# Bias addition and row maximum of the biased attentions in one VectorE instruction per token tile

## What is computed

```
a, b:  logits = q . k * 64**-0.5 + bias[head, bucket(t - s)],  -1e30 where s > t
l:     logits = q . k * 96**-0.5,                              -1e30 where s > t
p = softmax(logits);  o = p @ v            (b: p0 - lambda * p1)
```

## Time and profile before

| | before |
|---|---|
| median of three runs | 1180.93 us (1180.62 to 1181.59) |
| profiled execution, span from first to last instruction | 1175.5 us |
| around the span, against that median | 5.4 us |
| TensorE matmuls busy | 1127.3 us (96%) |
| VectorE busy | 746.6 us (64%), 997 instructions |
| ScalarE busy | 570.9 us (49%), 761 instructions |
| mean granted TensorE clock | 0.992 |

### The profile page before, as it was taken

One profiled execution on the slowest core, in us unless ns is written; L12 is line 12 of the kernel. 1 busy time (PEld: TensorE's weight loads), 2 busy tenths in 40 slices (PEclk: granted clock), 3 DMA queues, 4 the chain that ended last, 5 costly groups with the idle time before them and its releaser, 6 DMA issues.

```text
span 1175.5 us, 22572 instructions
## 1 busy us (share of the span) xinstructions
PE 1127.3 (96%) x9889; PEld 1071.8 (91%) x9889; DVE 746.6 (64%) x997; ACT 570.9 (49%) x761; POOL 76.0 (6%) x137
## 2 busy tenths in 40 slices
PE   7999999999999999999799999999998989999998
PEld 7787879879999999988688999999986789999998
DVE  4656867357465556767888756555587675665563
ACT  5445556344444434585345544343475554544443
POOL 2221011100000000400000000000020000000000
PEclk9999999999999999999899999999999999999999
DMA  6953354424555555534000555455554215455551
GB/s 253 337 160 108 144 180 180 149 102 173 179 187 180 180 183 193 192 141 144 1 3 3 184 180 188 180 180 184 190 201 143 73 60 188 183 180 180 181 189 61
DMA packets 30238, 185.04 MB, mean 157 GB/s; under 512 B 3579, under 2 KB 6848, under 8 KB 9148
## 3 DMA queue, kind: packets, MB, share of 16 engines
q1 hardware_dynamic: 24464, 174.07, 41.2%
q0 software_dynamic: 2464, 7.11, 2.1%
q10 hardware_dynamic: 3212, 2.42, 0.7%
HBM read 180.18 MB, written 3.41 MB: 156 GB/s over the span
## 4 chain that ended last, share of the span: by engine, by line
PE 75%; DVE 9%; ACT 6%; issue 4%; DMA 3%; POOL 2%; ACTq 0%; SPq 0%; DVEq 0%; POOLq 0%
PE bank L664 74%; ACT w_hi L2184 2%; DVE w_lo L1411 2%; DMA w_raw<-in_weights 2%; ACT exps L2284 1%; DMA bias<-bias_rows 1%; DVE stats L1606 1%; PE bank L843 1%; DVE logits L1598 1%; DVE inverse L2074 0%; PE bank L678 0%; DVE inverse_t L2099 0%; DMA bias_rows<-bias_lines 0%; POOL inverse_rms_diagonals L2672 0%; PE bank L1105 0%
## 5 line engine op out<-in xcount | busy, mean ns | idle before, releaser
L1411 DVE TENSOR_TENSOR w_lo<-w_raw,w_hi 128x2048 fp32r<-128x2048 f32 x160 | 364.8, 2291 | 194.7 <-ACT w_hi L2184 194.5
L2184 ACT ACTIVATE w_hi<-w_raw 128x2048 fp32r<-128x2048 f32 x164 | 312.0, 1913 | 110.7 <-DMA w_raw<-in_weights 105.2
L664 PE MATMUL bank<-x_channels_hi,w_hi 128*128 128x256 f32 x1424 | 231.7, 286 | 9.1 <-ACT w_hi L2184 3.5
L664 PE MATMUL bank<-x_channels_lo,w_hi 128*128 128x256 f32 x1424 | 229.1, 284 | 0.0
L664 PE MATMUL bank<-x_channels_hi,w_lo 128*128 128x256 f32 x1424 | 221.0, 278 | 0.0
L664 PEld LDWEIGHTS bank<-x_channels_hi,w_hi 128*128 128x128 f32 x1424 | 196.8, 192 | 12.5 <-ACT w_hi L2184 3.8
L664 PEld LDWEIGHTS bank<-x_channels_lo,w_hi 128*128 128x128 f32 x1424 | 194.9, 191 | 0.0
L664 PEld LDWEIGHTS bank<-x_channels_hi,w_lo 128*128 128x128 f32 x1424 | 191.5, 189 | 0.0
L664 PE MATMUL bank<-hidden_hi,w_lo 128*128 128x256 f32 x528 | 103.3, 284 | 0.0
L664 PE MATMUL bank<-hidden_hi,w_hi 128*128 128x256 f32 x528 | 102.0, 280 | 0.0
L664 PE MATMUL bank<-hidden_lo,w_hi 128*128 128x256 f32 x528 | 101.7, 279 | 0.0
(11 more groups left out here) (436 smaller groups left out, 1546.8 us busy)
## 6 DMA issues: line engine op xcount, KB each, us to landing
w_raw<-in_weights SPq DMA_DIRECT2D x164, 1024.0 KB, 4.8
bias_rows<-bias_lines POOLq DMA_DIRECT2D x3, 768.0 KB, 4.4
mem_rows<-in_mem POOLq DMA_DIRECT2D x2, 1024.0 KB, 5.2
bias<-bias_rows ACTq DMA_DIRECT2D x1, 1536.0 KB, 14.1
xn<-in_x SPq DMA_DIRECT2D x1, 1024.0 KB, 4.9
out<-xn SPq DMA_DIRECT2D x4, 256.0 KB, 2.5
wide_masks<-in_triangle_masks POOLq DMA_DIRECT2D x1, 832.0 KB, 6.5
bias<-bias_rows ACTq DMA_DIRECT2D x1, 768.0 KB, 5.5
```

What stands on the lines that cost most here:

```text
L664: return nc.tensor.matmul(out, lhs, rhs, start=start, stop=stop)
L1411: V.tensor_tensor(k.w_lo[:, s, :], k.w_raw[:, s, :], k.w_hi[:, s, :].bitcast(F32), ALU.subtract).then_inc(k.lo_done, 1)
L2184: A.activation(k.w_hi[:, s, :], k.w_raw[:, s, :], ACT.Copy).then_inc(k.hi_done, 1)
```

## The change

The two steps of VectorE become one instruction per token tile, `tensor_tensor_reduce`: out = (logits + bias) * (-scale), and beside it the minimum of `out` along the columns, started at 3e38, into `stats`. The stored logits are therefore negated, and the minimum is the negated maximum that the exponentials take as their bias; their scale becomes -1. Since the scale now multiplies the bias too, the one-hot matrix is multiplied by 8 when ScalarE copies it (64**-0.5 = 1/8); the mask -1e30 stays large whatever its factor, in "l" as well. The signal `biased` is gone: its waits, of TensorE before it overwrites a logits bank and before the turns of "mem" and after "b" and "l", are for `maxed`. The wait for the output of head h-4, which frees the `stats` slot, now stands ahead of the bias addition. The unbiased attentions keep their code.

```diff
@@ tensor_program, attention (twice) @@
-                    PE.wait_ge(*(k.biased if bias else k.exped).at(tag, i - 2))
+                    PE.wait_ge(*(k.maxed if bias else k.exped).at(tag, i - 2))
...
@@ tensor_program (also .all("b"), .all("l")) @@
-            turns("mem", (0, 1), k.biased.at("a", 6), k.biased.at("a", 7), k.mem_normed.all("mem"))
+            turns("mem", (0, 1), k.maxed.at("a", 6), k.maxed.at("a", 7), k.mem_normed.all("mem"))
...
@@ vector_program, attention, maxima @@
                 b, scale = bank[4 + h % 2], k.scale_of(tag)
+                if h >= 4 and step == 1:
+                    V.wait_ge(*k.o.at(tag, h - 4))
                 if bias:
                     if h >= 2:
                         V.wait_ge(*k.exped.at(tag, h - 2))
-                    L = k.lbuf[:, h % 2, 0:total]
...
-                    V.scalar_tensor_tensor(out=L, in0=b[:, 0:total], scalar=scale, in1=k.head_bias(tag, h), op0=ALU.mult,
-                                           op1=ALU.add).then_inc(k.biased.sem, 1)
-                    V.wait_ge(*k.biased.at(tag, h))
+                    for tok in range(NT):
+                        cols = slice(off[tok], off[tok] + spans[tok])
+                        r = V.tensor_tensor_reduce(out=k.lbuf[:, h % 2, cols], in0=b[:, cols], in1=k.head_bias(tag, h)[:, cols],
+                                                   scale=-scale, scalar=HUGE, op0=ALU.add, op1=ALU.min,
+                                                   accum_out=stat(h)[:, tok:tok + 1])
+                        if tok == 0:
+                            k.dve.mark(r)
+                    r.then_inc(k.maxed.sem, 1)
+                    continue
...
@@ scalar_program, attention, exponentials @@
-                                     scale=1.0 if bias else k.rstd_cols("cross")[:, tok:tok + 1] if tag == "c" else k.scale_of(tag),
+                                     scale=-1.0 if bias else k.rstd_cols("cross")[:, tok:tok + 1] if tag == "c" else k.scale_of(tag),
...
@@ scalar_program @@
-    A.activation(k.hot_r[:, :], k.hot[:, :], ACT.Copy).then_inc(k.act_once.sem, 1)
+    A.activation(k.hot_r[:, :], k.hot[:, :], ACT.Copy, scale=8.0).then_inc(k.act_once.sem, 1)
```

More of the change, by code:

```diff
@@ L23 @@
 NEG = -1e30
+HUGE = 3e38
 EPS = 1e-6
@@ L285, in signals @@
         self.qk = Signal(nc, "logits_made", **heads)
-        self.biased = Signal(nc, "logits_biased", **{n: heads[n] for n, a in att.items() if a[2]})
         self.maxed = Signal(nc, "logits_maxed", **heads)
@@ L828, in attention @@
                     if h >= 2:
-                        PE.wait_ge(*(k.biased if bias else k.exped).at(tag, h - 2))
+                        PE.wait_ge(*(k.maxed if bias else k.exped).at(tag, h - 2))
                 for tok in range(NT):
@@ L942, in tensor_program @@
     attention("b", beside_b)
-    PE.wait_ge(*k.biased.all("b"))
+    PE.wait_ge(*k.maxed.all("b"))
     PE.wait_ge(*k.pt.all("b"))
@@ L1136, in tensor_program @@
     attention("l", lambda i: warm(8, 0) if i == 0 else None)
-    PE.wait_ge(*k.biased.all("l"))
+    PE.wait_ge(*k.maxed.all("l"))
     PE.wait_ge(*k.pt.all("l"))
@@ L1597, in maxima @@
                         V.wait_ge(*k.pool_once.all("causal"))
-                    V.scalar_tensor_tensor(out=L, in0=b[:, 0:total], scalar=scale, in1=k.head_bias(tag, h), op0=ALU.mult,
-                                           op1=ALU.add).then_inc(k.biased.sem, 1)
-                    V.wait_ge(*k.biased.at(tag, h))
-                else:
[L1602 to L1616, removed]
+                    for tok in range(NT):
[5 more added lines that the diff above has]
+                            k.dve.mark(r)
@@ new lines, in maxima @@
+                    r.then_inc(k.maxed.sem, 1)
+                    continue
+                for tok in range(NT):
+                    r = V.tensor_reduce(out=stat(h)[:, tok:tok + 1], in_=b[:, off[tok]:off[tok] + spans[tok]], axis=AX.X,
+                                        op=ALU.max, negate=True)
+                    k.dve.mark(r)
+                V.wait_ge(*k.dve.so_far())
+                if tag == "c":
+                    V.wait_ge(*k.rstd_done.all("cross"))
+                    r = V.tensor_tensor(stat(h)[:, 0:2], stat(h)[:, 0:2], k.rstd_cols("cross"), ALU.mult)
+                else:
+                    r = V.tensor_scalar(stat(h)[:, 0:2], stat(h)[:, 0:2], scale, None, ALU.mult)
```

## The result

| | before | after |
|---|---|---|
| median (lowest to highest) | 1180.78 us (1179.04 to 1182.44), 6 runs | 1173.53 us (1171.42 to 1179.26), 6 runs |
| profiled execution's span, granted clock | 1175.5 us, 0.992 | 1171.9 us, 0.991 |
| VectorE busy | 746.6 us, 997 instructions | 732.9 us, 1025 instructions |

The forecast was 4.2 us less, 1176.7, with 1175.2 as the lower end of its range: the direction was right, and the gain was larger than the range allowed.

What follows compares the result with a forecast made beforehand. TensorE, busy 96% of the span, was taken to bound the kernel, so VectorE savings count only where TensorE waits. Gains of 2.2 ("l"), 1.0 ("a") and 1.0 ("b") sum to 4.2 us: 1180.93 to 1176.7 us, range 1175.2 to 1181.0.

Steps and rivals of the forecast that it cites:

- Instruction times: VectorE's new instruction in the 28 biased heads: 0.27 us for 128 columns, 0.42 us for 256.
- the scan-rate rivals: Fused instruction at scan rate: reads overlapped, 1180.3 us, chance 0.13; reads overlapping nothing, slower at 1184.5 us, chance 0.11.
- The read row: VectorE's one-column result as a row of its own, 0.16 us long, the next start 0.07 us later.
- "no separate read" price: Rival: no separate read rows on VectorE, 0.60 us won per head, 1176.2 us in all; chance 0.13.
- d: Time won per biased head in VectorE's pair of steps: 1.21 - 0.77 = 0.44 us.
- Effect in "l": In "l" the first and last links win 0.44 us each and four middle waits 0.33 each: 2.2 us.
- 1.96 us of other work: In "l", TensorE's work between head 3's logits and its transposes, after which it idles 0.33 us.
- Effect in "a": In "a", TensorE's waits shrink: `proj` 0.44 us, `qT_b` 0.44, `kT_b` 0.1; sum 1.0 us.
- Effect in "b": In "b", 0.25 us at the late products and the whole 0.8 us `cross_kT` wait; sum 1.0 us.
- Moved wait, scales: TensorE's later permit to overwrite logits banks, and the new scales in exponentials and one-hot copy, cost nothing.
- Nothing around the span: The 5.4 us between profiled span and median time lie around the span and stay untouched.
- a gain above 6 us: Sign of being wrong: such a gain would mean VectorE bounds places read as TensorE's.

Runs made afterwards that it cites:

- the repeat of the changed kernel: The changed kernel run once more, unaltered, beside variants of it: 1174.13 us beside 1181.22 for the kernel before, ratio 0.9939.
- the repeat: The kernel before, run again unchanged: 1181.68 us, ratio 1.0005; its profiled span was 1182.0 us.
- test 4: Changed kernel plus one more VectorE instruction per head, in "l": 1175.78 us; in "a" and "b" instead: 1175.17 us.
- test 6: Kernel before's separate additions and maxima, but per token tile, with the first tile's exponentials started early: 1175.23 us, ratio 0.9945 to the kernel before.

## Why the prediction was right and wrong, by its steps

1. *Instruction times*: right (0.27 and 0.42 forecast, 0.29 and 0.42 measured), and the scan-rate rivals fell. The Trainium skill's rule that a stage reading its own previous result has no bubble ("DVE: opcode table, instruction layouts, handler registers and perf-mode slots", Datapath and trigger behaviour) agrees with the trace, 134 ns for 128 more columns. The Trainium skill's warning on two non-bf16 SBUF sources ("Vector Engine (DVE) Microarchitecture Reference", Points that are easy to get wrong) is not tested here, as one source is in PSUM. *The read row*: there, but taken from the reciprocal at 0.07 and 0.16 us on the path; it costs nothing there. This is the "no separate read" price, d = 0.60, though the rows exist: d was 0.57. The Trainium skill ("VectorE: DVE Perf Modes", Two Vector instructions with no wait between them) counts an instruction that writes its accumulator as two, and the 56 rows agree; it gives no price.
2. *Effect in "l"*, the step that failed most: "With d above 0.33 TensorE itself bounds the loop: each pair of heads wins 0.33, not d." The term was 4 x 0.33 with 0.44 at either end, 2.2; measured is 0.57 ahead of the first transposes and five periods of 0.56, 3.37 (3.35 by the stage rows). The cap was read from the idle time of the matmul row alone. The weight loads showed 1.15 us of waiting per pair, and the floor lies 0.97 below (4.28 - 3.31): d = 0.57 was never near it. The "1.96 us of other work" from 929.99 to 931.95 held waiting too, since two heads of TensorE's own work are 3.31 us and not 4.28 - 0.33. The last head is in the right place; the first win comes one head earlier than the text had it, at head 0, whose wait fell from 0.78 to 0.22 us while head 1's stayed at 0.33, which leaves the sum as it was.
3. *Effect in "a"*: 1.0 forecast, 1.8 measured. `proj`: the forecast took d alone. ScalarE's second head had also waited for VectorE: its exponentials began 1.12 after the first head's before, and 0.89 after it now, so 0.57 + 0.23 = 0.80 was won. `qT_b`: 0.44 forecast, 0.38 measured. `kT_b`: "its second half may not start before TensorE's product ends" at 90.47, so 0.1. That time was the end of the value products which stand behind the product; the product itself had ended by 89.5. `kT_b` moved by 0.63 more and its wait fell from 0.9 to 0.2.
4. *Effect in "b"*: 1.0 forecast, 1.6 measured. Both places were right. The late pass went (12.66 to 12.36 us from the first logits of "b" to the second, 0.30). Another 0.26 went after it (7.26 to 7.00 us to the third), where the matmul row had shown no wait, but a weight load had waited 0.22 for the earlier `cross_kT` copy (the same load in the repeat of the changed kernel, at 122.42, waits for nothing):

```profile
124.87 0.53 PEld L664 LDWEIGHTS bank<-mem_channels_hi,w_hi 128*128 128x128 f32 x4 [0.22 <-DVE cross_kT L1493]
```

And the `cross_kT` wait at 141.25 was worth more than it showed. TensorE of the kernel before, then of the changed one (its repeat), in order of time:

```profile
139.63 0.83 PE L664 MATMUL bank<-proj,weights_t 128*128 128x128 f32 x6
141.25 1.20 PE L664 MATMUL bank<-w_hi,mem_channels_hi 128*128 128x512 f32 x4 [0.78 <-DVE cross_kT L1493]
```

```profile
137.19 0.83 PE L664 MATMUL bank<-proj,weights_t 128*128 128x128 f32 x6
137.78 1.17 PE L664 MATMUL bank<-w_hi,mem_channels_hi 128*128 128x512 f32 x4
```

From start to start it was 1.62 and is 0.59: a stall shown as 0.78 had cost 1.03. Again the matmul row's idle understates it.
5. *Moved wait, scales*: nothing, as forecast; the own-semaphore order shows in no wait. *Nothing around the span*: right for the change, wrong as a description: 1.3 us lie around it, and the other 4.1 go with the profiled execution's clock (0.992 against 0.985 in the repeat). Subtracting the gain from the median was right all the same.
6. The text named its own sign of being wrong: a gain above 6 us would mean that VectorE bounds places read as TensorE's. The gain was 7.25, and test 4 shows such a place in "l".

## What to carry to other kernels

Before capping a gain by TensorE's idle time, read the weight loads' waits too, and compare start-to-start distances with an unstalled stretch; then write down the loop of waits and count how often the latency stands in it. Compare kernels stage by stage from anchors that both have, and leave out stages with a half-speed stretch: that resolves 0.1 us where whole runs scatter by 2 to 8. And when a dependence is by tile, signal by tile: it gave another 3 us here, and even without the fused instruction most of the gain.

## What was not expected of the hardware

The accumulator read on VectorE overlaps the next instruction wholly (83 ns, start at the same hundredth); ScalarE's own (0.19 us) starts ahead of the next activation by 0.09. A half-speed stretch of 3.4 us cost 1.0 to 1.5 us in "a" and "b" here. With one source in PSUM and one in SBUF, the fused instruction and the plain addition ran at one rate: 286 and 284 ns for 128 columns, 420 and 416 for 256 (the plain ones in test 6).
